# The last feed-forward layer of a three-block network on unnormalised activations, the norm's factor applied at the eviction of its up products

## The reference

```python
def rmsnorm(x, g):
    y = xf * lax.rsqrt(jnp.mean(xf * xf, axis=-1, keepdims=True) + RMS_EPS)
    return (y * g.astype(jnp.float32)).astype(x.dtype)

def conv_glu_ffn(h, w_up, conv_w, conv_b, w_down):
    z = h @ w_up                      # 1024 -> 2 * 2816
    z1 = shift_prev(z)                # one token back
    z2 = shift_prev(z1)
    z = conv_w[0] * z2 + conv_w[1] * z1 + conv_w[2] * z + conv_b
    gate, val = jnp.split(z, 2, axis=-1)
    return (jax.nn.silu(gate) * val) @ w_down
```

## Time and profile before

| | us |
|---|---|
| median of three runs | 2151.45 |
| the runs | 2143.9, 2151.45, 2174.91 |
| span of the profiled execution | 2150.0 |

### The profile page before, as it was taken

The page is one execution under the profiler, slowest core; times in us unless marked ns, Lnnn a source line. Parts: engine busy times, 40 slices in busy tenths (PEclk is TensorE's granted clock), DMA queues, the critical chain, the costliest instruction groups (busy, mean ns, idle before and its releaser), DMA issues.

```text
span 2150.0 us, 47664 instructions
## 1 busy us (share of the span) xinstructions
PE 2122.7 (99%) x19346; PEld 2057.3 (96%) x19346; DVE 1437.0 (67%) x1972; ACT 1158.6 (54%) x1579; POOL 477.9 (22%) x254
## 2 busy tenths in 40 slices
PE   9999999999999999999999999999999999999998
PEld 8989999999999999988999999997999999999998
DVE  5666888657887899756899766567523454557554
ACT  6624655656666444664544544466544554556565
POOL 0030000100000355131354344310144400001443
PEclk9999999999999999998999999999999999999999
DMA  7223666444675787542788588644355453444552
GB/s 273 86 29 147 234 253 234 161 153 168 250 271 187 289 336 302 213 155 97 272 326 314 214 307 310 243 171 151 138 195 185 174 209 139 154 161 177 190 192 107
DMA packets 64391, 438.95 MB, mean 204 GB/s; under 512 B 7127, under 2 KB 9848, under 8 KB 12170
## 3 DMA queue, kind: packets, MB, share of 16 engines
q1 hardware_dynamic: 60480, 430.75, 54.0%
q10 hardware_dynamic: 3786, 6.38, 1.3%
HBM read 434.49 MB, written 2.62 MB: 203 GB/s over the span
## 4 chain that ended last, share of the span: by engine, by line
PE 91%; DVE 3%; ACT 3%; issue 1%; POOL 1%; DMA 0%; POOLq 0%; DVEq 0%
PE ps L346 25%; PE ps L348 25%; PE ps L347 25%; PE ps L360 1%; PE ps L368 1%; PE ps L362 1%; PE ps L1674 1%; PE ps L491 1%; PE ps L388 1%; ACT w_hi L284 1%; PE ps L390 1%; PE ps L389 1%; POOL hf L475 1%; PE ps L484 1%; PE ps L1696 1%
## 5 line engine op out<-in xcount | busy, mean ns | idle before, releaser
L346 PE MATMUL ps<-h_hi,w_hi 128*128 128x256 f32 x3412 | 956.3, 280 | 2.2 <-DVE h_lo L2442 1.3
L347 PE MATMUL ps<-h_lo,w_hi 128*128 128x256 f32 x3412 | 949.9, 278 | 0.0
L348 PE MATMUL ps<-h_hi,w_lo 128*128 128x256 f32 x3412 | 949.8, 278 | 0.0
L290 DVE TENSOR_TENSOR w_lo<-ring,w_hi 128x2048 fp32r<-128x2048 f32 x272 | 623.7, 2294 | 375.9 <-ACT w_hi L284 371.9
L284 ACT ACTIVATE w_hi<-ring 128x2048 fp32r<-128x2048 f32 x334 | 639.1, 1914 | 147.3 <-PE ps L348 142.7
L346 PEld LDWEIGHTS ps<-h_hi,w_hi 128*128 128x128 f32 x3412 | 644.6, 189 | 9.3 <-issue 6.5
L348 PEld LDWEIGHTS ps<-h_hi,w_lo 128*128 128x128 f32 x3412 | 644.9, 189 | 0.0
L347 PEld LDWEIGHTS ps<-h_lo,w_hi 128*128 128x128 f32 x3412 | 644.0, 189 | 0.2
L346 PE MATMUL ps<-g_hi,w_hi 128*128 (+1 forms) x1232 | 342.1, 278 | 1.6 <-POOL g_lo L894 0.9
L347 PE MATMUL ps<-g_lo,w_hi 128*128 (+1 forms) x1232 | 341.8, 277 | 0.0
L348 PE MATMUL ps<-g_hi,w_lo 128*128 (+1 forms) x1232 | 341.8, 277 | 0.0
(11 more groups left out here) (475 smaller groups left out, 2534.0 us busy)
## 6 DMA issues: line engine op xcount, KB each, us to landing
ring<-in_weights SPq DMA_DIRECT2D x334, 1024.0 KB, 4.8
mix<-in_modw SPq DMA_DIRECT2D x72, 1024.0 KB, 4.8
bias_rows<-below_mix ACTq DMA_DIRECT2D x1, 1536.0 KB
mix<-in_c_ssd ACTq DMA_DIRECT2D x1, 1536.0 KB, 8.1
x<-in_x SPq DMA_DIRECT2D x2, 512.0 KB, 3.8
ring<-in_weights SPq DMA_DIRECT2D x2, 512.0 KB, 6.5
mix<-in_c SPq DMA_DIRECT2D x2, 512.0 KB, 5.6
mix<-bias_rows ACTq DMA_DIRECT2D x1, 1024.0 KB, 8.4
```

Source lines behind the costliest of these rows:

```text
L290: dve.tensor_tensor(w_lo[:, n % SLOTS], ring[:, n % SLOTS], w_hi[:, n % SLOTS], ALU.subtract).then_inc(lo_ready[n % SLOTS], 1)
L346: pe.matmul(o, w[0], a_hi, start=first, stop=False, **kw)
L347: pe.matmul(o, w[0], a_lo, start=False, stop=False, **kw)
L348: return pe.matmul(o, w[1], a_hi, start=False, stop=last, **kw)
```

## The change

It concerns ffn6 (`scaled`) and the final norm.

- The norm of ffn6 is no longer applied to x. ACT makes h_hi from x times gain directly, in the order of tiles 0, 1, 4, 5, 6, 2, 3, 7, and squares x beside it (`scaled_act`). Tiles 2 and 3 wait until PE is done with the last unit of the stage before, which still reads them. DVE makes h_lo from x, gain and h_hi (`scaled_dve`). POOL adds seven of the eight squares' tiles down to two (`scaled_pool`, six additions for three before).
- PE starts the first up unit as soon as tiles are there, in the same order (`scaled_order`), with no `norm_pe` before it. The sums over channels (eight small products) stand behind unit 0, into bank 6, and the spreading of the factor stands in the middle of unit 1.
- ACT copies the spread factor to rstd. From then on an up product is evicted by DVE: zs = bank times rstd for both halves. acc is made by ACT from zs.
- The order of DVE in an up unit is now: zs, the low part of unit n+3 (odd and even m), then, once acc is done, the four taps, then the gate product. PE's bank is free when zs is made.
- Behind fin3's factor PE issues 32 products of 256 columns that nobody uses (`last_products`) where two warm-up products stood.

The other feed-forward layers keep their instructions; the set `dve_glo` names the layers in which DVE makes g_lo and has the same members as `dve_alone`. The diff, without the declarations (`acc_done` is a new semaphore, `scaled` holds ffn6 alone) and without the lines that change no instruction:

```diff
@@ -353,7 +356,7 @@
             pe.wait_ge(lo_ready[n % SLOTS], n // SLOTS + 1 + i)
             s = n % SLOTS
             if parts:
-                for k in range(ks):
+                for k in scaled_order(parts, ks):
                     pe.wait_ge(*after(f"act:{parts}.hi{k}"))
                     for b in range(2):
                         c, o = (2 * k + b) * P, ps[bank][:, b * T:(b + 1) * T]
@@ -426,6 +429,46 @@
             if split:
                 norm_act_parts(act, tag, kb, shift, dst)
 
+        def scaled_order(tag, ks):
+
+            return (0, 1, 4, 5, 6, 2, 3, 7) if tag in scaled and tag == "ffn6" else range(ks)
+
+        def scaled_act(act, tag, eps, gain, prev_last):
+
+            for q, (k, n) in enumerate(square_tiles(tag, KD)):
+                act.wait_ge(*after(f"dve:{STAGES[STAGES.index(tag) - 1]}.res{q}"))
+                for b in range(k, k + n) if tag != "ffn6" or q not in (1, 3) else () if q == 1 else (6, 2, 3):
+                    if tag == "ffn6" and b == 2:
+                        act.wait_ge(unit_done, prev_last + 1)
+                    act.activation(h_hi[:, b], x[:, b], ACT.Copy, scale=gain(b)).then_inc(*step(f"act:{tag}.hi{b}"))
+                act.activation(hf[:, k:k + n], x[:, k:k + n], ACT.Square).then_inc(*step(f"act:{tag}.sq{q}"))
+            act.activation(root[:, 2:3], eps_at[eps], ACT.Sqrt)
+
+        def scaled_pool(pool, tag):
+
+            for name, a, b, waits in (("pair0", 0, 1, ("act:{}.sq0",)), ("pair1", 2, 3, ("act:{}.sq1",)),
+                                      ("quad", 0, 2, ("pool:{}.pair0", "pool:{}.pair1")), ("pair2", 4, 5, ("act:{}.sq2",)),
+                                      ("six", 0, 4, ("pool:{}.quad", "pool:{}.pair2")), ("pair3", 6, 7, ("act:{}.sq3", "act:{}.sq4"))):
+                for w in waits:
+                    pool.wait_ge(*after(w.format(tag)))
+                pool.tensor_tensor(hf[:, a], hf[:, a], hf[:, b], ALU.add).then_inc(*step(f"pool:{tag}.{name}"))
+
+        def scaled_pe_sums(pe, tag):
+
+            for k, w in ((0, "six"), (6, "pair3")):
+                pe.wait_ge(*after(f"pool:{tag}.{w}"))
+                done = token_sums(pe, ps[6], k, lambda c: slice(c, c + 1), ones[:, 0:1], int(k == 0), k == 6)
+            done.then_inc(*step(f"pe:{tag}.ss"))
+
+        def scaled_dve(dve, tag, gain):
+
+            for q in range(4):
+                for b in (2 * q, 2 * q + 1):
+                    dve.wait_ge(*after(f"act:{tag}.hi{b}"))
+                    done = dve.scalar_tensor_tensor(out=h_lo[:, b], in0=x[:, b], scalar=gain(b), in1=h_hi[:, b],
+                                                    op0=ALU.mult, op1=ALU.subtract)
+                done.then_inc(*step(f"dve:{tag}.lo{q}"))
+
         def square_tiles(tag, kb):
 
             return [(0, 2), (2, 2), (4, 2), (6, 1), (7, 1)] if tag in STAGES else [(k, 2) for k in range(0, kb, 2)]
@@ -464,11 +507,14 @@
                 act.activation(rstd[:], ps[2][:, 0:T], ACT.Copy).then_inc(*step(f"act:{tag}.over1"))
 
         def norm_banks(tag):
-            return (2, 3) if tag in ("mla.kv", "mla.q") else (4, 7) if tag in ("ffn1", "ffn5") else (0, 7) if tag in STAGES else (6, 7)
+            return (6, 7) if tag in scaled else (2, 3) if tag in ("mla.kv", "mla.q") else (4, 7) if tag in ("ffn1", "ffn5") else (0, 7) if tag in STAGES else (6, 7)
 
         def norm_pool(pool, tag):
 
             if tag in TWICE:
+                return
+            if tag in scaled:
+                scaled_pool(pool, tag)
                 return
             for q in range(3):
                 pool.wait_ge(*after(f"act:{tag}.sq{q}"))
@@ -510,7 +558,22 @@
             if tag == "ev":
                 pe.wait_ge(load_sem("first"), 16)
             norm_pe_over(pe, tag)
-            keep_warm(pe, 2, warm, tag)
+            if tag.startswith("fin"):
+                last_products(pe)
+            else:
+                keep_warm(pe, 2, warm, tag)
+
+        def last_products(pe):
+
+            for j in range(8):
+                pe.matmul(ps[1][:, 0:T], w_hi[:, 0, P * (j // 4):P * (j // 4) + P], h_hi[:, j], start=True, stop=True)
+            for j in range(8):
+                pe.matmul(ps[1][:, 0:T], w_hi[:, 0, P * j:P * j + P], w_lo[:, 0, T * (j // 2):T * (j // 2) + T], start=True, stop=True)
+            for j in range(8):
+                r = slice(64 * (j % 2), 64 * (j % 2) + 64)
+                pe.matmul(ps[1 + j % 2][:, 0:T], w_hi[r, 0, P * (j // 2):P * (j // 2) + P], h_hi[r, j // 2], start=True, stop=True)
+            for j in range(8):
+                pe.matmul(ps[1][:, 0:T], w_hi[:, 0, 0:P], h_hi[:, 0], start=True, stop=True)
 
         def norm_pe_twice(pe, tag, sums, warm):
 
@@ -781,7 +844,12 @@
                         pe.wait_ge(z_free, zbase[name] + m - 1 + i * 2)
                     else:
                         pe.wait_ge(g_done, 22 * f + m - 1 + i * 2)
-                a_unit(pe, n, m % 2, i, parts=parts if m == 0 else None)
+                if m == 0 and name == "ffn1" and name in scaled:
+                    pe.wait_ge(*after("dve:dil.res4"))
+                a_unit(pe, n, m % 2, i, parts=parts if m == 0 else None,
+                       mid=(lambda: norm_pe_over(pe, name)) if m == 1 and name in scaled else None)
+                if m == 0 and name in scaled:
+                    scaled_pe_sums(pe, name)
 
             def down(j, n, i):
                 pe.wait_ge(glo_done, 22 * f + 2 * j + 2 + i * 2)
@@ -796,17 +864,27 @@
 
             def up(m, n, i):
                 e = m % 2
-                act.wait_ge(unit_done, n + 1 + i * 3)
+                c = nconv[name] if conv else 0
+                if name in scaled:
+                    act.wait_ge(z_free, zbase[name] + m + 1 + i * 2)
+                    if 22 * c + m >= 2:
+                        act.wait_ge(g_done, 22 * f + m - 1 + i * 2)
+                else:
+                    act.wait_ge(unit_done, n + 1 + i * 3)
                 if conv:
-                    c = nconv[name]
-                    if 22 * c + m >= 2:
+                    if 22 * c + m >= 2 and name not in scaled:
                         act.wait_ge(taps_done, 4 * (22 * c + m - 1) + i * 8)
-                    act.activation(zs[:, e], ps[e][:].rearrange("p (a b) -> p a b", a=2), ACT.Copy)
+                    if name not in scaled:
+                        act.activation(zs[:, e], ps[e][:].rearrange("p (a b) -> p a b", a=2), ACT.Copy)
                     for half in range(2):
-                        done = act.activation(acc[:, e, half], ps[e][:, half * T:(half + 1) * T], ACT.Identity,
+                        src = zs[:, e, half] if name in scaled else ps[e][:, half * T:(half + 1) * T]
+                        done = act.activation(acc[:, e, half], src, ACT.Identity,
                                               scale=vat("fcw" + name[3:], 88 + 22 * half + m + i * 2),
                                               bias=vat("fcb" + name[3:], 22 * half + m + i * 2))
-                    done.then_inc(z_free, 1)
+                    if name in scaled:
+                        done.then_inc(acc_done, 1)
+                    else:
+                        done.then_inc(z_free, 1)
                     if m < KF - 1:
                         hi(act, n + SLOTS, i)
                     act.wait_ge(taps_done, 4 * (22 * c + m + 1) + i * 8)
@@ -839,7 +917,17 @@
                 if conv:
                     c = nconv[name]
                     k = 4 * (22 * c + m)
-                    dve.wait_ge(z_free, zbase[name] + m + 1 + i * 2)
+                    if name in scaled:
+                        if m == 0:
+                            dve.wait_ge(*after(f"act:{name}.over"))
+                        dve.wait_ge(unit_done, n + 1 + i * 3)
+                        dve.tensor_tensor(zs[:, e], ps[e][:].rearrange("p (a b) -> p a b", a=2), by_block(rstd[:], 2),
+                                          ALU.mult).then_inc(z_free, 1)
+                        if m < KF - 1:
+                            lo(dve, n + SLOTS, i)
+                        dve.wait_ge(acc_done, 22 * scaled.index(name) + m + 1 + i * 2)
+                    else:
+                        dve.wait_ge(z_free, zbase[name] + m + 1 + i * 2)
                     for half in range(2):
                         dve.scalar_tensor_tensor(out=acc[:, e, half, 1:T], in0=zs[:, e, half, 0:T - 1],
                                                  scalar=vat("fcw" + name[3:], 44 + 22 * half + m + i * 2),
@@ -851,8 +939,10 @@
                                                  scalar=vat("fcw" + name[3:], 22 * half + m + i * 2),
                                                  in1=acc[:, e, half, 2:T], op0=ALU.mult,
                                                  op1=ALU.add).then_inc(taps_done, 1)
-                if m % 2 == 0:
+                if m % 2 == 0 and name not in scaled:
                     lo(dve, n + SLOTS, i)
+                if name in scaled:
+                    products(m, i)
```

(25 more changed lines are left out.)

9 lines of the change are left out of this document (7 added, 2 removed).

## The result

| | us |
|---|---|
| before, median of 6 runs | 2154.39 (2143.9 to 2174.91) |
| changed kernel, median of 6 runs | 2195.36 (2186.14 to 2204.22) |
| span of the profiled execution, before / after | 2150.0 / 2195.3 |

The ratio is 1.0175 with a 95% interval of 1.0124 to 1.0227. The kernel is slower; whether by more than 2% the runs don't tell.

A forecast was written before the change was run, and what follows sets the result against it. PE, busy 99%, bounded the kernel; a serial ACT-DVE chain would raise ffn6's turn from 16.32 to 20.50 us. The last down unit 44.3 later plus 1.6 for clock, added to 2151.45, gave 2197 us; range 2180 to 2206.

The forecast's parts named there:

- The bound and the serial chain: ffn6 loop: PE bounds before; afterwards zs, acc, high, low, taps, silu, gate run serially, turn 20.50 us against 16.32.
- rival A: Loop's even up units: POOL's and DVE's splits overlap, 10.10 us instead of 11.86, total 2181.5; chance 0.07.
- The eviction: DVE's new PSUM times rstd in each up unit: 0.69 us, less 0.08 overlap.
- The start: Start of ffn6: PE gains net 4.5 us, but the chain behind the first eviction starts only 0.55 us earlier.
- the step on POOL's additions: Norm of ffn6: POOL's three more additions lie under unit 0, at no cost.
- The end: Last down unit starts 44.3 us later, after a 4.8 us stall; low clock behind it adds 1.6 us.
- The clock in the loop: ffn6 loop: short half-clock stretches after stalls, hidden by PE's spare 4.2 us a turn.
- Rival C: Stalls keep PE at half clock throughout the loop, turn 30.5 us, total about 2285; chance 0.04.
- Releasers: PE idles before each down unit with POOL's g_lo as releaser, and not before ups in the loop.
- The tail and the range: The 32 final products cost nothing, 1 us at half clock; time 2180 to 2206, 0.57 for slower by 2%.
- Rival B: High and low parts leave the serial chain, PE stays the bound, start's 4.5 us gain remains: 2147; chance 0.05.
- The lock before the change: Old loop order: POOL's split ran while DVE was idle, so their mutual exclusion cost nothing.

The follow-up runs named there:

- e1: Changed kernel with DVE's low parts of ffn6 back in their two old places; median 2151.5 us, ratio 0.9935 to the kernel before.
- e4: Kernel before with DVE's new order alone (low part of unit n+3 ahead of the taps in ffn6); one run, 2192.31 us.
- e3: Changed kernel with POOL's low parts of ffn6's down weights shrunk to one column; one run, 2179.89 us.
- e5: Changed kernel with two warm-up products back in place of the 32 behind fin3's factor; one run, 2204.23 us.
- e8: Second trace of e1, the changed kernel with DVE's old order; one run, 2155.56 us.
- b1: Kernel before, unchanged, profiled again; span 2128.7 us.
- b2: Kernel before, unchanged, profiled once more; span 2139.5 us.
- e7: e1 without POOL's additions of squares and with h_lo ahead of the second half of unit 1's low part; median 2152.21 us.

## Why the prediction was right, point by point

- **The bound and the serial chain: right.** The odd up unit was put at 8.64 us and took 8.74, the even one at 11.86 and took 11.86, the turn at 20.50 and took 20.60. e1 and e4 show that the order does it, and e3 that the lock is 1.7 us of it (1.76 was forecast for rival A).
- **The eviction: right.** 0.69 was taken from the residual addition, and 0.68 to 0.69 measured. The pair of acc was undersized: the start of acc to the start of the high part is 1.00 us against 0.89, inside the 1.01 that bounded it, and the hand-over from zs is 0.26 (2010.67 + 0.68 to 2011.61) against 0.21. Together that is 0.16 for each up unit that POOL's lock does not cover, some 2 us over the layer; the odd up unit as a whole is 0.10 over its forecast. High part to low part (1.93) and low part to taps (2.21) were right within 0.03.
- **The start: the step on POOL's additions failed.** They were said to lie under unit 0 and to cost nothing. They lie there, but hold the same lock as h_lo, which took 4.70 us and not 3.2. This trace reaches ffn6 1.06 us earlier than the one before, so the first acc at 1966.32 is 1.4 us later than the 1965.95 forecast, and instead of 0.55 us earlier than before it is 0.9 later. The prediction had applied the lock to the weight splits and not to these. The start also rests on a draw: 1.1 us of the gain that was forecast for it is the low clock behind the norm's gap, which two of the three traces of the kernel before don't have. Against those the first acc is 2.0 us later.
- **The end: two errors that cancel, in this trace.** The last down unit was to start 44.3 us later. It starts 45.2 us later in the traces and 46.3 if the 1.06 are counted. The 1.6 us for a low clock behind its stall did not come here: the stall is 1.99 us long and not 4.8, the granted clock is 1.00 (2180.00:2182.00), and the first residual piece follows after 1.69 us as before (1.68). In e5, the same program up to there, it did come: a stall of 4.23 us, the clock at 0.50 behind it, and 1.27 us lost. So the term is there in some executions and absent in others. 45.9 was forecast in sum, and the span moved by 45.3; that the two lie so close is in part luck, since the medians of six runs moved by 41.0.
- **The clock in the loop: right in kind.** It is 0.92 in the loop, so there are low stretches, and the turn doesn't show them. They take up part of the idle time that was put at 4.2 us a turn, of which 2.5 us are left (20.8 us in the 170). DVE waits for TensorE 0.74 us at 2020.24, under the shadow of POOL's split. Rival C, the clock at half for the whole loop, did not come.
- **Releasers: one was wrong.** I said that g_lo would come last before the down units. It is the down unit's own low part by POOL (24.5 of the 30.9 us), since the g that it takes is two up units old. Only before the last down unit is it g_lo. The time is the same, as POOL's split hangs on the same chain.
- **The tail and the range: right.** Measured median 2195.36 in 2180 to 2206. On the side of 2% the forecast had 0.57 for slower; the measured ratio lies just under, with both sides in its interval.
- **Rival B** (the 4.5 us at the start remain) falls even where its condition is made. In e8 the chain is under TensorE's time, and the first down unit starts 26.58 us behind the third residual piece, against 28.54 in the trace that the forecast was made from: of the 4.5 us forecast 1.96 are there. 1.5 went to the late h_lo (TensorE's sums begin at 8.60 us and not 7.1); the other 1.0 is not assigned. Against b1 and b2 (27.40 and 27.41) only 0.8 us are there. The late low part (1.08) and the end (1.95) cost more than that.
- **The lock before the change:** the prediction says that it cost nothing in the old order, and in time that holds. It was met there too, though, the other way round. While DVE's low part ran from 2118.29 to 2120.57, POOL's g_lo took 2.04 us instead of 0.74 and ended 0.60 after it, and POOL's split began 0.39 us behind the end of the high part. The prediction put this hand-over at 0.03; in the changed kernel it is 0.08 (2019.96 + 1.90 to 2021.94). The two rows of before:

```profile
2118.29 2.28 DVE L290 TENSOR_TENSOR w_lo<-ring,w_hi 128x2048 fp32r<-128x2048 f32 x1
...
2119.13 2.04 POOL L894 TENSOR_TENSOR g_lo<-gf,g_hi 128x256 f32 x1 [4.11 <-ACT g_hi L820]
```

## What to carry to other kernels

Moving an operation forward in one engine's queue also moves everything behind it back to what that operation waits for. If what it waits for is made by the engine that waits for the results behind it, two half-empty engines become one chain; add up the chain for a turn and compare it with the bounding engine's time before moving anything. Where two engines exclude each other on SBUF, an operation that was harmless because the other was idle then must be priced again after every reordering, small additions too.

## What the runs showed of the hardware that I had not expected

TensorE's products of 256 columns start 0.1133 or 0.1178 us apart, 4%, at a granted clock of 1.00 in both cases, for stretches of up to some 200 us, in the same place differently from one execution to the next. Three traces of one program spanned 2128.7, 2139.5 and 2150.0 us. Between the first two most of the difference is this rate (in 400.00:690.00, at a granted clock of 1.00 in both, 2577 products are recorded in the one and 2485 in the other); between the last two it is mostly the granted clock, at 0.50 for some 20 us in one of them (8.2 of 10.5 us). A trace that is compared with another has to be compared on the product rate and the granted clock first.

The lock, by which a DVE operation with two SBUF operands and an operation of POOL keep each other waiting, has the shape that the prediction read out of one row, and more of it could be seen. A low weight part that meets POOL's split ends 2.14 or 2.15 us after the split, whether it came 1.8 or 2.8 us into it; alone it takes 2.29. An eviction, which reads PSUM and one SBUF tile, is not held up (0.69 at 2020.24 above, beside POOL's g_lo below, both of their normal length, and 0.69 at 2125.57 in e8, inside the split of 2124.98 to 2129.61), and the taps, which read two SBUF tiles, are, as in e7, where a pair of them takes 3.72 us beside the split instead of 0.88:

```profile
2020.25 0.75 POOL L990 TENSOR_TENSOR g_lo<-gf,g_hi 128x256 f32 x1 [8.00 <-ACT g_hi L898]
```

```profile
2001.53 3.72 DVE L929 SCALAR_TENSOR_TENSOR acc<-zs,vec,acc 128x255 f32<-128x255 f32 x2 [1.52 <-ACT acc L880]
...
2010.67 0.88 DVE L929 SCALAR_TENSOR_TENSOR acc<-zs,vec,acc 128x255 f32<-128x255 f32 x2 [1.49 <-ACT acc L880]
```

The Trainium skill, SBUF — State Buffer, section SBUF: two separate sides, makes just this distinction, by two SBUF inputs on DVE's side; the traces agree with it.
